# A gated delta rule whose state meets the raw keys: values corrected on VectorE, T applied once per chunk

## The reference

```python
tri = where(strict, beta_i * kk * decay, 0) + eye            # T = tri^-1
rhs = concatenate([v * beta, k * (beta * exp(G))], axis=-1)
u, w = split(triangular_solve(tri, rhs))                     # u = T (beta v),  w = T (beta e^G k)
def step(S, ...):                                            # one chunk, S is 128 x 128
    v_new = u_c - w_c @ S
    o = (q * e^G) @ S + (q k^T * decay) @ v_new
    S = chunk_decay * S + (k * e^(G_last - G))^T @ v_new
```

## Time and profile before

| | |
|---|---|
| median of 3 runs | 1327.15 us (1326.84 to 1327.43) |
| profiled execution | 1327.31 us, span 1325.4 us |
| PE busy | 1301.2 us, 98% of the span |
| DVE busy | 759.3 us, 57% |
| ACT busy | 622.0 us, 47% |
| granted TensorE clock | 0.999 |
| mixer | from about 32 to 331 us of the span |
| one period of the loop | 35.40 us |

### The profile page before, as it was taken

How to read it: one execution, slowest core, us unless ns; L and a number is a source line. 1 busy time by engine, 2 the same in 40 slices (tenths; PEclk the granted TensorE clock), 3 DMA queues, 4 the chain that set the end, 5 groups by cost and what they waited for, 6 DMA issues and landing times.

```text
span 1325.4 us, 21907 instructions
## 1 busy us (share of the span) xinstructions
PE 1301.2 (98%) x8445; PEld 1061.1 (80%) x8445; DVE 759.3 (57%) x1193; ACT 622.0 (47%) x988; POOL 0.2 (0%) x4
## 2 busy tenths in 40 slices
PE   6999999999999999999999999999999999999998
PEld 4778888888788888888887777778888888888886
DVE  7777877874753443443465867676443433434555
ACT  6766667765542241332455677644431422314342
POOL 0000000000000000000000000000000000000000
PEclk9999999999999999999999999999999999999999
DMA  4232322322333233333334122225333333332333
GB/s 160 79 94 62 75 76 79 64 81 65 112 96 111 82 109 95 95 95 96 95 96 159 48 72 72 78 66 166 92 108 90 102 96 95 99 99 87 95 92 100
DMA packets 41297, 123.56 MB, mean 93 GB/s; under 512 B 4048, under 2 KB 11664, under 8 KB 40720
## 3 DMA queue, kind: packets, MB, share of 16 engines
q1 hardware_dynamic: 33472, 116.88, 29.4%
q10 hardware_dynamic: 7760, 5.80, 2.2%
HBM read 118.44 MB, written 4.23 MB: 93 GB/s over the span
## 4 chain that ended last, share of the span: by engine, by line
PE 90%; DVE 5%; ACT 2%; issue 1%; DMA 1%; SPq 0%; DVEq 0%; ACTq 0%
PE acc L376 26%; PE acc L378 26%; PE acc L377 26%; DVE work L1988 1%; PE ps L867 1%; DVE wl L352 1%; DMA work<-rows 1%; DMA raw<-in_weights 1%; ACT wh L345 1%; PE ps L593 1%; PE ps L544 1%; PE ps L666 1%; PE ps L477 1%; PE ps L639 1%; PE ps L840 1%
## 5 line engine op out<-in xcount | busy, mean ns | idle before, releaser
L376 PE MATMUL acc<-xh,wh 128*128 128x512 f32 x1008 | 408.2, 405 | 9.0 <-DVE xl L2171 9.0
L378 PE MATMUL acc<-xh,wl 128*128 128x512 f32 x1008 | 394.0, 391 | 0.0
L377 PE MATMUL acc<-xl,wh 128*128 128x512 f32 x1008 | 393.8, 391 | 0.0
L345 ACT ACTIVATE wh<-raw 128x1024 fp32r<-128x1024 f32 x207 | 216.9, 1050 | 181.3 <-DMA raw<-in_weights 167.3
L352 DVE TENSOR_TENSOR wl<-raw,wh 128x1024 fp32r<-128x1024 f32 x207 | 252.9, 1222 | 58.0 <-ACT wh L345 54.9
L376 PE MATMUL acc<-yh,wh 128*128 128x512 f32 x608 | 237.4, 391 | 0.0
L377 PE MATMUL acc<-yl,wh 128*128 128x512 f32 x608 | 236.6, 389 | 0.0
L378 PE MATMUL acc<-yh,wl 128*128 128x512 f32 x608 | 236.6, 389 | 0.0
L376 PEld LDWEIGHTS acc<-xh,wh 128*128 128x128 f32 x1008 | 189.9, 188 | 48.7 <-DVE wl L352 9.3
L378 PEld LDWEIGHTS acc<-xh,wl 128*128 128x128 f32 x1008 | 189.6, 188 | 40.6
L377 PEld LDWEIGHTS acc<-xl,wh 128*128 128x128 f32 x1008 | 190.1, 189 | 36.0 <-issue 1.2
(11 more groups left out here) (274 smaller groups left out, 1093.1 us busy)
## 6 DMA issues: line engine op xcount, KB each, us to landing
raw<-in_weights SPq DMA_DIRECT2D x208, 512.0 KB, 3.5
work<-rows ACTq DMA_DIRECT2D x14, 256.0 KB, 6.8
h<-in_xT SPq DMA_DIRECT2D x4, 512.0 KB, 6.9
proj<-work ACTq DMA_DIRECT2D x2, 1024.0 KB, 4.1
work<-proj SPq DMA_DIRECT2D x2, 1024.0 KB, 7.1
outT<-h SPq DMA_DIRECT2D x8, 256.0 KB, 2.6
cst<-in_cst SPq DMA_DIRECT2D x1, 512.0 KB, 5.7
work<-in_pT SPq DMA_DIRECT2D x1, 512.0 KB, 4.6
```

Source lines behind the costliest of these rows:

```text
L345: nc.scalar.activation(slot(u)[0][:], raw[u.const % 2][:], ACT.Copy).then_inc(hi_done, 1)
L376: nc.tensor.matmul(dst[:], hi, mh[:, k, :], start=(n == 0), stop=False)
L377: nc.tensor.matmul(dst[:], hi, ml[:, k, :], start=False, stop=False)
L378: mm = nc.tensor.matmul(dst[:], lo, mh[:, k, :], start=False, stop=(n == KT - 1))
```

## The change

w = T (beta e^G k) is no longer formed. Since u - w S = T (beta v - beta e^G (k S)), the state is multiplied by the raw keys, DVE subtracts the scaled product from the values, and T is applied once.

- PE: step w and its 3 matmuls go. New steps: `keys` (only pe_ktr), `v0` (T vb for chunk 0, and pe_kk), `ks(c)` (k S and the state's part of the output), `td(c)` (T times the corrected values). The steps of one period go from 16 to 19, and the lists of fills are rewritten.
- DVE: `correct(c)`, three times in a period, a 128x128 scalar_tensor_tensor that adds -beta e^G (k S) to `vb`. The order becomes state(0), yl, correct(0), beta, state(1), correct(1), lt, state(2), take_head, correct(2), split of the fourth unit, pairs, ti, taps, split of the fifth unit. One table gets its sign turned at the start (L1573).
- ACT: the 3 copies into `kb` and the copy into `nw` go; one 128x512 copy of the keys into `kst` comes at the head of the period.

```diff
-            def w():
-                pe.wait_ge(ttl_d, i * 3)
-                ...
-                for c in range(1, C):
-                    last = nc.tensor.matmul(ch(ps[1], c), ch(kb, c), ch(TT, c), start=True, stop=True)
-                last.then_inc(w_d, 1)
+            def keys():
                 if ahead:
                     pe_ktr(pe, i + 1)
+            def v0():
+                pe.wait_ge(vb_d, i)
+                pe.wait_ge(ttl_d, i * 3)
+                nc.tensor.matmul(ch(ps[3], 0), ch(TT, 0), ch(vb, 0), start=True, stop=True).then_inc(v_d, 1)
+                if ahead:
+                    pe_kk(pe, i + 1)
+            def ks(c):
+                ...
+                    pe.wait_ge(s_d, b * 3 + c)
+                    nc.tensor.matmul(ch(ps[1], c), ch(kst, c), S, start=True, stop=True).then_inc(ks_d, 1)
+                    nc.tensor.matmul(ch(ps[5], c), S, ch(qd, c), start=True, stop=False)
+            def td(c):
+                    pe.wait_ge(v0_d, b * 3 + c)
+                    nc.tensor.matmul(ch(ps[3], c), ch(TT, c), ch(vb, c), start=True, stop=True).then_inc(v_d, 1)
+                    if c == QK_AT_CHUNK and early:
+                        pe_qk(pe, i)
-            return ([x(0), tx(0), vtr, x(1), tx(1), x(2), tx(2), w] + [s for c in range(C) for s in (v(c), os(c))]
+            return ([x(0), tx(0), vtr, x(1), tx(1), x(2), tx(2), keys, v0, os(0)]
+                    + [s for c in range(1, C) for s in (ks(c), td(c), os(c))]
-        FILL = [3, 3, 0, 3, 3, 3, 3, 2, 1, 2, 1, 2, 1, 2, 1, 2]
-        FIRST_FILL = [3, 3, 0, 2, 3, 2, 3, 2, 1, 1, 1, 2, 1, 2, 2, 2]
-        SHORT_FILL = [2, 2, 0, 2, 2, 2, 2, 2, 1, 2, 1, 1, 1, 1, 1, 2]
-        LAST_FILL = [1, 2, 0, 1, 2, 1, 2, 1, 1, 1, 2, 1, 2, 1, 2, 5, 10]
+        FILL = [3, 3, 0, 3, 3, 3, 3, 2, 1, 1, 1, 1, 1, 1, 1, 1, 1, 1, 2]
+        FIRST_FILL = [3, 3, 0, 2, 3, 2, 3, 2, 1, 1, 1, 1, 1, 1, 1, 1, 1, 1, 2]
+        SHORT_FILL = [2, 2, 0, 2, 2, 2, 2, 1, 1, 1, 1, 1, 1, 1, 1, 1, 1, 1, 1]
+        LAST_FILL = [1, 2, 0, 1, 2, 1, 2, 0, 1, 1, 1, 1, 1, 1, 1, 1, 1, 1, 6, 10]
-                    act.wait_ge(w_d, b)
-                    if c > 0:
-                        ins = nc.scalar.activation(ch(kb, c), ch(ktoks[b % 2], c), ACT.Copy, scale=tc(2, c, b))
+            nc.scalar.activation(kst, kcs[0], ACT.Copy).then_inc(k_state, 1)
-            act_nw(act, i)
+            def correct(c):
+                dve.wait_ge(ks_d, b * 3 + c + 1)
+                ...
+                nc.vector.scalar_tensor_tensor(out=ch(vb, c + 1), in0=ch(ps[1], c + 1), scalar=tc(2, c + 1, b),
+                                               in1=ch(vb, c + 1), op0=ALU.mult, op1=ALU.add).then_inc(v0_d, 1)
             if ahead:
                 dve_knorm(dve, i + 1)
+            state(0)
             if b > 0:
                 dve_yl(dve, b)
-            state(0)
+            correct(0)
             if ahead:
                 dve_beta(dve, i + 1)
+            state(1)
+            correct(1)
+            if ahead:
                 dve_lt(dve, i + 1)
-            state(1)
+            state(2)
             if early:
                 dve_take_head(dve, 2, i)
+            correct(2)
+            if early:
                 split_lo(dve, Unit(first + 3))
-            state(2)
```

More of the change, by code:

```diff
@@ L180, in build @@
         Tts, TT0, Xe = [W(16)[:, 0:P], W(16)[:, P:2 * P]], W(16)[:, 2 * P:3 * P], W(16)[:, 3 * P:3 * P + HD]
-        TT, Xl, kb, kd, vb = W(17), W(18)[:, 0:C * HD], W(19), W(20), W(21)
-        nw, qd, vn, egs, osq, yb = W(22), W(23), W(24), [W(25), M(1)], W(26), W(27)
+        TT, Xl, kd, vb = W(17), W(18)[:, 0:C * HD], W(20), W(21)
+        kst, qd, vn, egs, osq, yb = W(22), W(23), W(24), [W(25), M(1)], W(26), W(27)
         ktoks, ksq = [M(2), M(3)], M(4)
@@ L483, in pe_qk @@
             if now(j):
-                pe.wait_ge(nw_d, j)
+                pe.wait_ge(v0_d, j * 3)
                 pe.wait_ge(k_kept, j)
@@ L622, in tx @@
                 return step
-            def w():
-                pe.wait_ge(ttl_d, i * 3)
-                if early:
-                    pe.wait_ge(te_d, i * 4 + 4)
-                pe.wait_ge(kbkd_d, i)
-                for c in range(1, C):
-                    last = nc.tensor.matmul(ch(ps[1], c), ch(kb, c), ch(TT, c), start=True, stop=True)
-                last.then_inc(w_d, 1)
+            def keys():
                 if ahead:
                     pe_ktr(pe, i + 1)
-            def v(c):
-                def step():
-                    if c == 0:
-                        pe.wait_ge(vb_d, i)
-                    last = nc.tensor.matmul(ch(ps[3], c), ch(TT, c), ch(vb, c), start=True, stop=(c == 0))
-                    if c > 0:
[L641 to L653, removed]
@@ new lines, in v0 @@
+            def v0():
[5 more added lines that the diff above has]
+            def ks(c):
+                def step():
+                    if c == 1:
+                        pe.wait_ge(k_state, i)
+                        pe.wait_ge(qd_d, i)
+                        if early:
+                            pe.wait_ge(te_d, i * 4 + 4)
+                        if not past:
+                            pe.wait_ge(qkd_d, 1)
+                    pe.wait_ge(s_d, b * 3 + c)
+                    nc.tensor.matmul(ch(ps[1], c), ch(kst, c), S, start=True, stop=True).then_inc(ks_d, 1)
+                    nc.tensor.matmul(ch(ps[5], c), S, ch(qd, c), start=True, stop=False)
+                return step
@@ L663, in step @@
                         pe.wait_ge(o1_d, b)
+                    if c == 0:
+                        pe.wait_ge(kbkd_d, i)
                     if c < C - 1:
@@ L697, in pe_out_steps @@
                 if unit is units[4]:
-                    pe.wait_ge(nw_d, H)
+                    pe.wait_ge(v0_d, H * 3)
                 for _ in range(KT - 1):
@@ L1187, in token_k @@
                 if b > 0:
-                    act.wait_ge(w_d, b)
                     act.wait_ge(su_d, b * 3)
[L1190 to L1193, removed]
-                        ins = nc.scalar.activation(ch(kb, c), ch(ktoks[b % 2], c), ACT.Copy, scale=tc(2, c, b))
+                for c in range(C - 1):
+                    ins = nc.scalar.activation(ch(kd, c), ch(ktoks[b % 2], c), ACT.Copy, scale=tc(3, c, b))
                 ins.then_inc(kbkd_d, 1)
@@ L1221, in act_gdn @@
                 rows_of(2)
+            if b > 0:
+                act.wait_ge(v_d, b * 4)
+                act.wait_ge(k_kept, b)
+            else:
+                act.wait_ge(k_silu, 1)
+            nc.scalar.activation(kst, kcs[0], ACT.Copy).then_inc(k_state, 1)
             if early:
@@ L1224, in act_gdn @@
                 act.wait_ge(qk_d, i)
+                act.wait_ge(k_state, i)
                 nc.scalar.activation(kcs[0], kcs[1], ACT.Copy).then_inc(k_kept, 1)
@@ L1572, in s3 @@
                 dve.wait_ge(g_act, 7)
-                nc.vector.tensor_tensor(tabs[:, 64:96], tabs[:, 64:96], tabs[:, 32:64], ALU.mult).then_inc(g_dve, 1)
+                nc.vector.scalar_tensor_tensor(out=tabs[:, 64:96], in0=tabs[:, 64:96], scalar=-1.0, in1=tabs[:, 32:64],
+                                               op0=ALU.mult, op1=ALU.mult).then_inc(g_dve, 1)
                 dve.wait_ge(g_pe, 4)
```

11 lines of the change are left out of this document (4 added, 7 removed).

## The result

The change makes the kernel slower. Over four runs each, the changed kernel took 1335.86 us (1334.73 to 1337.69) and the kernel before 1327.29 us (1326.84 to 1328.17): a ratio of 1.0062, interval 1.0046 to 1.0078. That is +8.6 us where +5.9 was forecast; 1335.86 lies in the range and near the upper end of the forecast's own, 1330 to 1337.

The account below looks back on a forecast made before the run. The prediction took TensorE, busy 98% of the span, to bound the kernel. Its terms, -5.4 + 0.5 + 7.1 + 1.7 + 0.5 + 1.5 = +5.9 us, gave a median of 1333.0 us; own range 1330 to 1337, 8-in-10 range 1325.5 to 1338.5.

Parts of the forecast that it names:

- removed matmuls: On TensorE, three matmuls per period (L630) go, 0.67 us in each of eight periods: -5.4 us.
- pace of the chunks: Per chunk, td to os ties with copying v; 0.03 us for each of 17 new places: +0.5 us.
- tx(0), periods 2 to 6: TensorE waits 0.80 us for VectorE's masks, whose chain moves back 2.28 us over a cover of 1.58: +4.0 us.
- tx(0), periods 7 and 8: The same wait for VectorE's masks in the periods with fewer fills: +1.5 us in period 7, +1.6 us in period 8.
- ks(1) of period 7: TensorE's ks(1) waits for state(0), since VectorE is still in the taps of q: +1.7 us.
- os(0) of period 8: os(0) moves forward, but ScalarE is in a split and then copies v: +0.5 us.
- the rows' DMA: Later issue delays decay and ks(1) in periods 2 to 6: between 0 and 3.7 us, taken as +1.5 us.
- Rival 1: The cover holds: no wait at tx(0) and the rows come in time; 1322.8 to 1324.5 us, chance 0.13.
- rival 2: Loop waits at tx(0) are 0.3 instead of 0.8 and the rows cost nothing: 1328 us, chance 0.15.
- Rival 3: The rows land early and the loop's ks(1) never waits: +4.4, 1331.5 us; chance 0.60 together with the forecast.
- Rival 4: A second chain of waits in every loop period, decay 1 us or more late: 1338 us and above, chance 0.12.

Follow-up runs that it names:

- pairs_early: Changed kernel with VectorE's lt ahead of correct(1), and pairs and ti between correct(1) and state(2), in periods 1 to 6: 1328.72 us, ratio 1.0005 to the kernel before.
- changed_again: The changed kernel once more, unedited, with a second profile: 1337.52 us, ratio 1.0073 to the kernel before.
- split_back: Changed kernel with take_head and the fourth unit's split back in front of state(2) on VectorE: 1335.77 us, ratio 1.005 to the kernel before.
- old_algorithm_new_order: The kernel before, with w, nw and its fills, and VectorE in the new order without corrections: 1333.24 us, ratio 1.0038 to the kernel before.
- fills_before_state: Changed kernel with SHORT_FILL giving two fill steps more ahead of ks(1), taken from the period's end: 1339.05 us, ratio 1.0083 to the kernel before.
- tiny_correct: Changed kernel with its three corrections per period replaced by a one-column copy behind the same waits: 1334.18 us, ratio 1.0047 to the kernel before.
- order_from_period2: Changed kernel with the order of pairs_early in periods 2 to 6 and the old place in period 1: 1330.09 us, ratio 1.0023 to the kernel before.
- head7_order: pairs_early with period 7's own order: state(0) ahead of q's taps on VectorE, v's second copy ahead of SiLU of q on ScalarE: 1324.56 us, ratio 0.9983.
- order_in_period1: Changed kernel with the order of pairs_early in period 1 alone: 1334.42 us, ratio 1.006 to the kernel before.
- head8_order: head7_order with, in period 8, v's copy ahead of ScalarE's split and state(0), dve_yl, correct(0) ahead of VectorE's split: 1323.33 us, ratio 0.9973.

## Why the prediction was right, and which terms were off

The balance of the profiled executions, in us. The wait is read from a bracket where there is one; the rest of an interval between two tx(0) is what the same interval of before, less 0.67 and the named waits, leaves over. The last term but the sum is tx(0) of period 1, which started at 60.76 instead of 61.46, and 0.5 behind the mixer.

| term | forecast | measured |
|---|---|---|
| removed matmuls | -5.4 | -5.4 |
| pace of the chunks | +0.5 | +1.2 |
| tx(0), periods 2 to 6 | +4.0 | +4.3 |
| tx(0), periods 7 and 8 | +3.1 | +1.4 and +1.5 |
| ks(1) of period 7 | +1.7 | +1.6 |
| os(0) of period 8 | +0.5 | +0.3 |
| the rows' DMA | +1.5 | +0.3 (second profile: about +1.3) |
| gap at L593, period 2 | none | +2.5 |
| half clock, period 8 | none | +1.5 |
| start of the mixer and behind it | none | -1.2 |
| sum | +5.9 | +8.0 (profiled: +8.3) |

**Removed matmuls.** Right. They show where no wait covers them, in `pairs_early`. The prediction's reading that the mixer had two waits for VectorE missed a third: x(0) of the first head (L544) waits 0.3 us ahead of period 1. It is 0.26 before and 0.23 after, and changes nothing.

**tx(0).** Right, to 0.06 us in each of the seven periods but one, where it was 0.1, and shown as a mechanism by its going when pairs moved. Rival 1, that the cover holds, is excluded, and so is rival 2: the starts on VectorE came within 0.03 us of the forecast, so operations overlap no more than their starts had shown. VectorE's 43% of idle time was no help, since the idle time arose inside the chain.

**ks(1) of period 7 and os(0) of period 8.** Right: 1.64 against 1.66 worked out, and 0.32 in the bracket against 0.5. With another order of work both waits went.

**The pace.** Mis-sized. The chunks of period 5 take 3.19 and 3.26 us, those of period 6 3.24 and 3.22, against 3.20 before, so td to os costs 0.03 on the mean as forecast. But with the waits set aside, periods 4 and 5 leave 0.15 us over, and eight of those are 1.2. `pairs_early` has the same remainder, 0.16 in a loop period without waits. In period 5, 0.06 of the 0.15 lies in its second chunk and 0.09 between su2 and tx(0) (9.69 less the wait of 0.86, against 8.74). What makes these 0.09 us was not settled.

**The rows' DMA.** In the first profile 0.3 instead of 1.5, of the forecast's terms the furthest off. The timeline of ScalarE and its queue after, against the earlier trace rows:

```profile
238.94 0.93 ACTq L1049 DMA_DIRECT2D work<-rows  x2
...
248.22 1.28 ACT L1071 ACTIVATE more<-work 128x128 f32<-128x128 f32 x4 [0.94 <-DMA work<-rows]
```

The issue came 2.89 us ahead of tx(0), where 2.8 was worked out (239.01 - 236.2), and the decay's wait grew from 0.66 to 0.94 as said. But the decay began 9.28 us after the issue, not 9.95. That is 0.67 less, and the prediction had the point from which the term is nothing at 0.7. The other four periods have 8.58 to 9.42, and ks(1) was late in one period of the loop only, the one with 9.42, by 0.12 us. One landing of before was taken for all, and it was the longest: its five periods have 9.16 to 9.95. Rival 3, the rows early and 1331.5 us, is what happened in this term, with the rest of the forecast as it was.

The second profile of the same kernel went the forecast's way. The timelines of ScalarE and TensorE in `changed_again`, period 4:

```profile
170.80 0.93 ACTq L1049 DMA_DIRECT2D work<-rows  x2
...
180.31 1.28 ACT L1071 ACTIVATE more<-work 128x128 f32<-128x128 f32 x4 [1.16 <-DMA work<-rows]
```

```profile
193.32 0.38 PE L666 MATMUL ps<-work 128*128 128x128 f32 x2
...
194.69 0.46 PE L645 MATMUL ps<-work 128*128 128x128 f32 x2
```

Here the decay began 9.51 us after the issue, and ks(1) came 1.37 us after os(0) instead of 1.14. Periods 3 and 6 have 9.62 and 9.74 and the same lateness, period 5 has 8.94 and none. So the chain from the rows to ks(1) exists as it was worked out. The three late periods leave 0.3 to 0.6 us each beyond the pace, 1.3 in all. The mechanism was right, and its size differs from one execution to the next.

Rival 4, a second chain of waits in every period, is excluded: where it asked for 1 us or more in each, ks(1) was late by 0.12 us in one period of the loop, and in the second profile by 0.23 in three. The total came near its 1338 all the same, through two things that no row of before holds: it has neither the gap nor, in the mixer, a stretch at half clock. These two are 4.0 us of the balance and the pace adds 0.7; the rows' DMA and the last term take back 2.4, smaller differences 0.2, and 0.3 us of the miss of 2.4 have no place in the balance. The loop's period was 264.75 - 228.88 = 35.87 us, forecast 35.9, partly by luck: less for the DMA, more for the pace. That the median lies inside the range of 1325.5 to 1338.5 has some luck in it too: with the same kernel measured again, two of four executions (1339.72 and 1340.38) lie above it.

## What to carry to other kernels

An engine's mean idle time says nothing on whether a new dependent operation fits; count from the last thing that it must wait for to the next thing that the bound engine needs, in the engine's own program order. Where an order makes an engine idle inside such a chain, move independent work into that idle time: here the same algorithm went from +8.6 us to no difference by moving pairs (5.7 us of waits, and most of the gap in period 2, which was not foreseen), and to -3.7 us once the two short periods had orders of their own. A transfer's one measured landing is a draw and not a price, and a term that rests on it deserves both ends.

## What the runs showed of the hardware

**A gap of TensorE that nothing in the kernel explains.** In the first period of the loop, inside the 32x32 matmuls of tx(1), TensorE stopped in the changed kernel as its timeline shows:

```profile
102.43 0.21 PE L593 MATMUL ps<-work 32*32 32x16 f32 x2
105.12 0.42 PE L593 MATMUL ps<-work 32*32 32x16 f32 x27 [2.48 <-issue]
```

The gaps were 2.48 and 2.22 in the changed kernel, 2.30, 1.75, 1.79, 2.33 and 2.29 in `split_back`, `old_algorithm_new_order`, `fills_before_state`, `tiny_correct` and `order_from_period2`, and 0.36, 0.16, 0.39 and 1.05 in `pairs_early`, `head7_order`, `order_in_period1` and `head8_order`, the four kernels with the order of `pairs_early` in period 1. Before has none. The DMA view of the changed kernel between 102.4 and 103 us has a line of its own for instructions:

```profile
q8 instruction: 1, 0.02, 9.7%
```

One packet of 16 KB of instructions starts there, at 102.80. In each of the eleven kernels and profiles with a gap TensorE went on 2.2 to 2.4 us after the start of such a packet, so the length of the gap is how late the packet was. Where the gap is 1.75 us or more, the packet started between 0.05 us ahead of tx(1)'s first matmul and 0.65 behind it; where it is 0.16 to 1.05, it started 0.8 to 1.6 us ahead, and in the kernel before 2.0 us ahead. That TensorE ran out of instructions fits all of this. What sets the moment of the fetch, and why VectorE's order in period 1 moves it, was not tried; the cause is argued from times so far, and not shown.

**Half clock behind a wait.** The windows of the changed kernel before and after tx(0) of period 8 (columns: us, busy time and instructions of PE, PEld, DVE, ACT, POOL, granted clock, DMA share, GB/s):

```profile
306.00:309.00 3.00, 1.46 (x37) 1.01 (x36) 2.94 (x10) 2.45 (x4) 0.00 (x0) 0.98 0.08 22
309.00:312.00 3.00, 3.00 (x25) 2.17 (x23) 2.05 (x5) 2.69 (x8) 0.00 (x0) 0.50 0.87 309
```

and the matmuls of 512 columns inside, on TensorE's timeline:

```profile
309.23 0.63 PE L376 MATMUL acc<-yh,wh 128*128 128x512 f32 x1
309.65 0.63 PE L377 MATMUL acc<-yl,wh 128*128 128x512 f32 x1
310.08 0.63 PE L378 MATMUL acc<-yh,wl 128*128 128x512 f32 x1
```

They start 0.43 us apart instead of 0.23: a granted clock of 0.50, the 1.2 GHz level, from 308.9 to 312.3, after three microseconds in which TensorE was busy for 1.46. This costs about 1.5 us on top of the wait itself: from tx(0) to os(0) period 8 takes 12.50 us here, and 11.00 in `changed_again`, which has no such stretch there. Such stretches, 3.4 or 6.8 us long, begin at or just behind the gap of period 2 in `changed_again` (6.8 us), `split_back` (6.8), `fills_before_state`, `old_algorithm_new_order` and `tiny_correct`, at tx(0) of period 7 in `changed_again`, and at tx(0) of period 8 in the first profile, in `pairs_early`, `order_from_period2` and `fills_before_state` (6.8). They do not follow every wait: `order_in_period1` has waits of 1.9, 1.6, 1.5 and 1.4 us in the mixer and no such stretch, and the changed kernel had one behind its gap in one profile and not in the other. Five kernels also have one in period 1, four of them behind the wait of 1.9 us that stands at its tx(0) in every kernel; the kernel before has that wait, one of 1.3 us too, and no such stretch. So a wait of 1.3 to 2.9 us here costs itself and, some of the time, 1.5 to 3 us more. That is the likely reason for most of the 3 us on top in `fills_before_state`, and it bounds what one profile can tell of such a kernel.
